# Two-block transformer, fp32, one core: passages between sublayers reordered, the mixer's last product held whole, gate units inside the attention

## The reference

```python
for l in range(DEPTH_2):
    x = x + 0.5 * rmsnorm_2(swiglu(rmsnorm_2(x, ffn1_pre_g[l]), w_ffn1_in[l], w_ffn1_out[l]), ffn1_post_g[l])
    h = rmsnorm_2(x, mix_pre_g[l])
    (z, xbc, dt_raw, rq, rk, rv, rg, aq, ak, av, gate) = jnp.split(h @ w_in[l], offsets, axis=-1)
    y_ssd = ssd_mixer(z, xbc, dt_raw, ...)
    y_ret = retention_mixer(rq, rk, rv, rg, ...)
    y_att = swa_sink_attention(aq, ak, av, ...)
    branch = jnp.einsum('blmc,mcd->blmd', ys, w_branch[l])
    gates = jax.nn.sigmoid((gate + b_gate[l]).reshape(bsz, L, N_BRANCH, D_MODEL))
    y = jnp.sum(gates * branch, axis=2) @ w_out[l]
    x = x + rmsnorm_2(y, mix_post_g[l])
    x = x + 0.5 * rmsnorm_2(swiglu(rmsnorm_2(x, ffn2_pre_g[l]), w_ffn2_in[l], w_ffn2_out[l]), ffn2_post_g[l])
```

## Time and profile before

| | |
|---|---|
| median of three executions | 2131.18 us |
| profiled execution | 2128.98 us, its span 2127.2 us |
| TensorE, matmuls | 1950.0 us busy, 92% |
| VectorE | 1150.1 us, 54% |
| ScalarE | 884.1 us, 42% |
| weights moved | 483 MB, 228 GB/s over the span |
| mean granted clock of TensorE | 0.946 |
| second block | from 621 us to the end |

### The profile page before, as it was taken

How to read it: one execution, slowest core, us unless ns; L and a number is a source line. 1 busy time by engine, 2 the same in 40 slices (tenths; PEclk the granted TensorE clock), 3 DMA queues, 4 the chain that set the end, 5 groups by cost and what they waited for, 6 DMA issues and landing times.

```text
span 2127.2 us, 29966 instructions
## 1 busy us (share of the span) xinstructions
PE 1950.0 (92%) x12346; PEld 1546.6 (73%) x12346; DVE 1150.1 (54%) x1583; ACT 884.1 (42%) x1288; POOL 47.5 (2%) x99
## 2 busy tenths in 40 slices
PE   7988766777779999999999999999999999999998
PEld 7873121121148887899899888898878999998887
DVE  5751100110137657477865676476674779656763
ACT  5521000000025444457744554354444577445552
POOL 0010000000000000000000100000000000001000
PEclk9988778777789999999999999999999999999999
DMA  7568999999995554543445455454545434355552
GB/s 280 194 262 327 421 421 421 421 421 421 421 368 176 213 186 171 184 158 120 149 159 180 180 193 185 177 178 182 195 178 186 170 120 149 140 181 188 188 191 87
DMA packets 66900, 486.05 MB, mean 228 GB/s; under 512 B 7424, under 2 KB 7424, under 8 KB 8544
## 3 DMA queue, kind: packets, MB, share of 16 engines
q1 hardware_dynamic: 65632, 476.25, 59.1%
q0 software_dynamic: 1152, 8.16, 1.0%
HBM read 483.33 MB, written 1.05 MB: 228 GB/s over the span
## 4 chain that ended last, share of the span: by engine, by line
PE 76%; DMA 10%; SPq 7%; DVE 3%; ACT 2%; issue 2%; POOL 1%; DVEq 0%; ACTq 0%; POOLq 0%
PE bank L1540 22%; PE bank L1555 12%; PE bank L1640 11%; DMA work<-in_w_experts 10%; PE bank L1873 8%; PE bank L1553 7%; SPq L1440 6%; PE bank L1569 3%; PE bank L1551 2%; PE bank L1368 2%; PE bank L1398 1%; PE bank L1421 1%; PE bank L1091 1%; ACT work L2319 1%; PE bank L2058 1%
## 5 line engine op out<-in xcount | busy, mean ns | idle before, releaser
L1518 DVE TENSOR_TENSOR ring_parts<-ring,work_parts 128x2048 fp32r<-128x2048 f32 x188 | 430.2, 2291 | 237.3 <-ACT work_parts L1511 223.1
L1511 ACT ACTIVATE work_parts<-ring 128x2048 fp32r<-128x2048 f32 x168 | 321.0, 1913 | 217.6 <-PE bank L1640 80.0
L1540 PE MATMUL bank<-work_parts 128*128 128x256 f32 x1376 | 317.6, 283 | 1.2 <-DVE ring_parts L1518 1.2
L1540 PE MATMUL bank<-rows_parts,work_parts 128*128 128x256 f32 x864 | 245.1, 284 | 0.0
L1540 PE MATMUL bank<-rows_parts,ring_parts 128*128 128x256 f32 x864 | 244.4, 283 | 0.0
L1540 PEld LDWEIGHTS bank<-work_parts 128*128 128x128 f32 x1376 | 238.9, 192 | 1.7 <-issue 1.5
L1555 PE MATMUL bank<-work_parts 128*128 128x512 f32 x840 | 213.2, 393 | 0.0
L1553 PEld LDWEIGHTS bank<-work_parts,ring_parts 128*128 128x128 f32 x1280 | 174.6, 190 | 12.3
L1398 PE MATMUL bank<-work 128*32 128x512 f32 x640 | 126.3, 886 | 59.2 <-DMA work<-in_w_experts 59.2
L1553 PE MATMUL bank<-work_parts,ring_parts 128*128 128x256 f32 x1280 | 178.5, 282 | 0.0
L1555 PEld LDWEIGHTS bank<-work_parts 128*128 128x128 f32 x840 | 150.1, 189 | 26.2
(11 more groups left out here) (387 smaller groups left out, 3150.7 us busy)
## 6 DMA issues: line engine op xcount, KB each, us to landing
ring<-in_w_layers SPq DMA_DIRECT2D x242, 1024.0 KB, 4.9
work<-in_w_experts SPq DMA_DIRECT2D x136, 1024.0 KB, 26.8
ring<-in_w_experts SPq DMA_DIRECT2D x48, 1024.0 KB, 26.7
ring<-in_w_first SPq DMA_DIRECT2D x16, 1024.0 KB, 5.5
columns<-in_w_experts SPq DMA_DIRECT2D x8, 1024.0 KB, 26.6
work<-in_post POOLq DMA_DIRECT2D x3, 1024.0 KB, 5.0
work<-in_second POOLq DMA_DIRECT2D x1, 2944.0 KB, 11.5
work<-in_first SPq DMA_DIRECT2D x1, 1805.5 KB, 11.3
```

Of the source, the lines that this page charges most:

```text
L1511: act.activation(his[j % len(his)], m.ring[U.slot(names[j])], ACT.Copy).then_inc(F["unit_hi"], 1)
L1518: dve.tensor_tensor(m.ring_r[slot], m.ring[slot], his[j % len(his)].bitcast(F32), ALU.subtract).then_inc(F["unit_lo"], 1)
L1540: mm = pe.matmul(out, w, x, start=k + n == 0, stop=k == KT - 1 and n == 2)
```

## The change

Six things are changed, in both layers of the second block:

- `bridge_vector`: rows of half 0 are scaled before bank (0,1) is read, and `next_columns(0)` comes before bank (1,1) is read; it came after x of half 1. One `OUT_ORDER` serves all three.
- `mx.out`: the mixer's last product holds all four units; half 0 is finished for both column halves, then half 1 (`out_rows`). Unit 0 of FFN 2 is taken apart after the passage and no longer before it.
- `mix_columns_vector`: the low part of a column is made straight from the bank by one fused instruction for each 128x128; the whole column is no longer stored, and the 16-row `dt` product, which read it, is split into three fp32r matmuls a step, with its weights taken apart too.
- The gate units `g.1.0` and `g.1.1` move into the two halves of the attention, and one unit more of the mixer's end is kept ahead (`END_AHEAD`), in four buffers instead of three.
- `turn_half(.., 1)`: the second half's transposes come later: in an FFN after 24 instead of 16 fp32 matmuls, in the mixer after 21 instead of 12 fp32r ones.
- `with_skips`: seven places of the job list stay empty in FFN 1, and the list's length is a multiple of eight.

```diff
+END_AHEAD = AHEAD_UNITS + 1
@@ place
+        if name is None:
+            continue
+SKIPPED = range(4, 18, 2)
+def with_skips(jobs):
+
+    return [n for job in jobs for n in ([None, job] if job in [f"f1.in.{i}.a" for i in SKIPPED] else [job])]
@@ LAYER_JOBS
-              + [f"ap.0.{kv}.{j}" for kv in range(2) for j in range(2)] + ["ao.0.0", "ao.0.1"]
-              + [f"ap.1.{kv}.{j}.{s}" for kv in range(2) for j in range(2) for s in range(2)] + ["ao.1.0", "ao.1.1"]
+              + [f"ap.0.{kv}.{j}" for kv in range(2) for j in range(2)] + ["g.1.0", "ao.0.0", "ao.0.1"]
+              + [f"ap.1.{kv}.{j}.{s}" for kv in range(2) for j in range(2) for s in range(2)] + ["g.1.1", "ao.1.0", "ao.1.1"]
+assert len(LAYER_JOBS) % BANKS == 0
+END_HOME = [(6, None, 4, 5)[j % 4] for j in range(14)] + [4, 3, 5, 6, None, 4]
@@ ffn_tensor
-    turn_half(pe, B, ps, m, F, f, 1)
     B.claim(pe, jobs[1])
-    whole_half(pe, B, U, ps, m, jobs[1], units[1], 0)
+    whole_half(pe, B, U, ps, m, jobs[1], units[1], 0, None, lambda: turn_half(pe, B, ps, m, F, f, 1))
@@ bridge_vector
-        if (n, t) == (1, 1):
+        if (n, t) == (0, 1):
             scaled(0)
+        elif (n, t) == (1, 1) and next_columns:
+            next_columns(0)
...
-    if next_columns:
-        next_columns(0)
     scaled(1)
@@ mix_tensor
+    def out_rows(held, ready):
+
+
+        for t in range(TT):
+            for n in range(2):
+                B.claim(pe, f"mx.out.{n}.{t}")
+        parts = {}
+        for u in range(2):
+            for n in range(2):
+                parts[n, u] = unit_parts(pe, m, U, F, "end", END_SPLIT, 16 + 2 * n + u, m.ehi_r, KT // 2)
+                part_rows(f"mx.out.{n}.0", parts[n, u], u, 0, held, ready if n == 0 else None)
+        for n in range(2):
+            part_rows(f"mx.out.{n}.1", parts[n, 0], 0, 1, held).then_inc(U.parts_sem, 1)
+            part_rows(f"mx.out.{n}.1", parts[n, 1], 1, 1, held)
...
-        mm = pe.matmul(ps[B.bank("dt")][0:16, 0:T], wdt[:, k, :], m.hT[:, k, :], start=k == 0, stop=k == KT - 1)
+        for n, (w, x) in enumerate(passes_of([w[:, k, :] for w in wdt], [x[:, k] for x in moving])):
+            mm = pe.matmul(split(ps[B.bank("dt")][0:16, 0:T], TT), w, x, start=k + n == 0, stop=k == KT - 1 and n == 2)
@@ attend
+        end_columns("g", 1, t, moving)
@@ mix_scalar
     for t in range(TT):
+        if t == 1:
+            gate(1, 0)
@@ mix_columns_vector
-        whole = dve.tensor_tensor(m.hT[:, c, tokens], half_of(ps, B, job, t), bc(m.lp["gmix"][:, c], [P, 2, P]), ALU.mult)
...
+        for k in range(2):
+            kk = 2 * i + k
+            ins = dve.scalar_tensor_tensor(out=m.mhlo_r[:, t, kk, :], in0=bank[:, k, :], scalar=m.lp["gmix"][:, kk:kk + 1],
+                                           in1=m.mh_r[:, t, kk, :].bitcast(F32), op0=ALU.mult, op1=ALU.subtract)
@@ mix_vector
+    bridge_vector(dve, m, ps, B, F, "mx", m.post[:, 0:D], 1.0, next_columns)
     for j in range(NEXT_UNITS["mx"]):
         next_unit(j)
-    bridge_vector(dve, m, ps, B, F, "mx", m.post[:, 0:D], 1.0, next_columns)
```

More of the change, by code:

```diff
@@ L1556, in wide_columns, with whole_half @@
         mm.then_inc(B.full(job), 1)
-def whole_half(pe, B, U, ps, m, job, unit, t, ready=None):
+def whole_half(pe, B, U, ps, m, job, unit, t, ready=None, between=None):
     pe.wait_ge(*U.landed(unit))
@@ L1564, in whole_half @@
     for c in range(2):
+        if between and c == 1:
+            between()
         out = ps[B.bank(job)][:, c * T + t * P:c * T + (t + 1) * P]
@@ L1721, in ffn_parts_scalar @@
         act.activation(m.both_r[:, :, tokens], m.hfull[:, :, tokens], ACT.Copy).then_inc(F["x_hi"], 1)
-OUT_ORDER = {"f1": ((0, 0), (1, 0), (0, 1), (1, 1)), "mx": ((0, 0), (0, 1), (1, 0), (1, 1)),
-             "f2": ((0, 0), (1, 0), (0, 1), (1, 1))}
+OUT_ORDER = ((0, 0), (1, 0), (0, 1), (1, 1))
 def squared(F, f, n, t):
-    return F.at(f"{f}.pss", OUT_ORDER[f].index((n, t)) + 1)
+    return F.at(f"{f}.pss", OUT_ORDER.index((n, t)) + 1)
 def bridge_scalar(act, m, ps, B, F, f, next_columns):
-    for n, t in OUT_ORDER[f]:
+    for n, t in OUT_ORDER:
         job = f"{f}.out.{n}.{t}"
@@ L1863, in mix_tensor, with part_rows @@
     moving = [x.rearrange("p t k n -> p k t n") for x in (m.mh_r, m.mhlo_r)]
-    def part_rows(job, parts, u, t, held, ready=None):
+    def part_rows(job, parts, u, t, held, ready=None, between=None):
         for k in range(KT // 2):
             kk = u * (KT // 2) + k
+            if between and k == KT // 2 - 1:
+                between()
             if ready and kk % 2 == 0:
@@ L1901, in split_rows_by_half @@
                     B.claim(pe, jobs[t])
-                mm = part_rows(jobs[t], parts[u], u, t, held, ready[t])
+                mm = part_rows(jobs[t], parts[u], u, t, held, ready[t], between if (t, u) == (0, 1) else None)
                 if (t, u) == (1, 0):
                     mm.then_inc(U.parts_sem, 1)
+    def out_rows(held, ready):
[10 more added lines that the diff above has]
+            part_rows(f"mx.out.{n}.1", parts[n, 1], 1, 1, held)
     turn_half(pe, B, ps, m, F, "mx", 0)
     split_rows_by_half(["rq.0", "rq.1"], "mx", MIX_SPLIT, 0, m.mhi_r, moving,
-                       [[F.at("mx.cols", 4 * t + i + 1) for i in range(4)] for t in range(TT)],
+                       [[F.at("mx.cols", i + 1) for i in range(4)], [B.drained(f"mx.n.{i}") for i in range(4)]],
                        lambda: turn_half(pe, B, ps, m, F, "mx", 1))
@@ L2081, in branch, with end_columns @@
             return
-        for n, (name, held) in enumerate((("g", moving), ("b", (m.yhi_r[b - 1], m.ylo_r[b - 1])))):
-            if n == 1:
-                pe.wait_ge(*F.at("end_lo", b))
-            for i in range(4):
-                job = f"{name}.{b}.{i}"
-                B.claim(pe, job)
-                parts = unit_parts(pe, m, U, F, "end", END_SPLIT, (b - 1) * 8 + n * 4 + i, m.ehi_r, KT)
-                split_columns(pe, B, ps, job, parts, held)
+        for i in range(2 if b == 1 else 0, 4):
+            end_columns("g", b, i, moving)
+        pe.wait_ge(*F.at("end_lo", b))
+        for i in range(4):
+            end_columns("b", b, i, (m.yhi_r[b - 1], m.ylo_r[b - 1]))
+    def end_columns(name, b, i, held):
+        job = f"{name}.{b}.{i}"
+        B.claim(pe, job)
+        parts = unit_parts(pe, m, U, F, "end", END_SPLIT, END_SPLIT.index(job), m.ehi_r, KT)
+        split_columns(pe, B, ps, job, parts, held)
     def attend(t):
@@ L2120, in mix_tensor @@
     branch(2)
-    summed = (m.yhi_r[0], m.sumlo_r)
-    split_rows(["mx.out.0.0", "mx.out.0.1"], "end", END_SPLIT, 16, m.ehi_r, summed,
-               [F.at("sum_lo", i + 1) for i in range(4)])
-    split_rows_by_half(["mx.out.1.0", "mx.out.1.1"], "end", END_SPLIT, 18, m.ehi_r, summed, (None, None), lambda: None)
+    out_rows((m.yhi_r[0], m.sumlo_r), [F.at("sum_lo", i + 1) for i in range(4)])
 def mix_unit_scalar(act, m, U, F, j):
@@ L2337, in end_unit @@
     def end_unit(j):
-        if j < len(END_SPLIT):
-            unit_hi(act, m, U, F, END_SPLIT, j, m.ehi_r)
-    act.wait_ge(*B.filled("b.0.1"))
+        if j >= len(END_SPLIT):
+            return
+        act.wait_ge(*B.filled(END_READ[j]))
+        act.wait_ge(*U.landed(END_SPLIT[j]))
+        act.activation(m.ehi_r[j], m.ring[U.slot(END_SPLIT[j])], ACT.Copy).then_inc(F["unit_hi"], 1)
     end_unit(0)
+    end_unit(1)
     for t in range(TT):
+        if t == 1:
+            gate(1, 0)
         for kv in range(2):
@@ L2349, in mix_scalar @@
                         turned_probs(act, m, ps, B, F, t, kv, j, s)
-    act.wait_ge(*B.filled("ap.1.1.1.1"))
-    end_unit(1)
+    end_unit(2)
     for b in (1, 2):
-        u = (b - 1) * 8 + AHEAD_UNITS
+        u = (b - 1) * 8 + END_AHEAD
         for i in range(4):
@@ L2361, in mix_scalar @@
                 act.activation(m.yhi_r[i], (m.yret, m.yatt)[i], ACT.Copy).then_inc(F["end_hi"], 1)
-            gate(b, i)
+            if (b, i) != (1, 0):
+                gate(b, i)
         for i in range(4, 8):
             end_unit(u + i)
-    for j in range(16 + AHEAD_UNITS, len(END_SPLIT)):
+    for j in range(16 + END_AHEAD, len(END_SPLIT)):
         end_unit(j)
+    bridge_scalar(act, m, ps, B, F, "mx", next_columns)
     for j in range(NEXT_UNITS["mx"]):
         next_unit(j)
-    bridge_scalar(act, m, ps, B, F, "mx", next_columns)
 def gates_of(m, i):
@@ L2849, in lay_out @@
     m.rv, m.aq, m.osqh = split(rv, TT), split(rv, KT), split(rv, 8)
+    m.wdt_r = [area_r[:, W.at + 1024 + i * P:W.at + 1024 + (i + 1) * P] for i in range(2)]
     rw = W.take(RET_H * 3 * P)
```

48 lines of the change are left out of this document (24 added, 24 removed).

## The result

| | before | after |
|---|---|---|
| median, six executions each | 2131.07 us (2127.7 to 2133.07) | 2111.71 us (2110.22 to 2115.69) |
| ratio | | 0.9913, 95% interval 0.990 to 0.9926 |
| profiled execution, its span | 2128.98, 2127.2 us | 2115.69, 2113.9 us |
| TensorE idle over 0.1 us at a time, behind the first transposes of the second block | 16.4 us | 7.2 us |
| low stretches (granted clock 0.50) between 650 us and the last product | 815.0 (6.8 us), 1183.7 (3.4), 1374.8 (3.4) | none |

A forecast was written before the change was run, and what follows sets the result against it. TensorE is busy 92%, so only idle gaps, low-clock stretches and matmul work could change the time. Terms summed to 9.0 us, 13.1 with the clock: 2131.18 to 2118; own range 2112 to 2122, 8 in 10 2111 to 2126.5.

The forecast's parts named there:

- into FFN 2, waits, two layers: Passage from mixer into FFN 2: idle falls from 2.51 to 0.55 us, 1.96 saved per layer, 3.9 in all.
- FFN 2 into FFN 1, waits: Layer 1's FFN 2 into layer 2's FFN 1: skipped places end the L1813 wait; idle 2.53 to 0.8, 1.7 us saved.
- mixer entry, waits, two layers: FFN 1 into the mixer: a new 1.8 us wait before the second transposes; 0.35 lost per layer, 0.7 in all.
- attention: Gate product between probability transposes and their product: 0.87 us gap goes, half 0's product shortens; 1.5 per layer, 2.9 saved.
- `dt` and what stands beside it: 16-row product: 24 fp32r matmuls replace eight fp32, 3.56 to between 2.7 and 3.0 us; 0.65 saved twice, 1.3.
- tail, behind the block: Very end: scaled rows stand ahead of two bank reads, x still waits for the root; 0.1 us lost.
- clock: Half-clock stretches after passages given back: 1.6 and 1.4 us, plus 1.1 of 2.5 at the mixer's entry; 4.1 together.
- The fit called "within 0.1": Mixer into FFN 2: half 1's scaled rows ready at T+6.4 us, its transposes asked for at T+6.5.
- the covered low part: Attention: VectorE's moved 2.29 us low part hides under the gate product; uncovered, its 2.29 would return in each layer.
- A: Rival, passages: idle goes but other passages, mostly the mixer's entry, take low-clock stretches; 9.0 saved, 2122 us; chance 0.21.
- B: Rival, five passages: half 1's x waits for columns, each losing another 1.5 us; 7.5 of 13.1 gone, 2125.5; chance 0.17.
- C: Rival, slower: low parts late at b.1.0 behind the attention, or held units late in the last product; 2136 and above; chance 0.04.

The follow-up runs named there:

- e3: Changed kernel with VectorE's old order in all five passages (half 0 scaled ahead of bank (1,1), next columns behind the update of x): 2128.12 us, ratio 0.9989.
- e2: Changed kernel with the mixer's last product in its old order (column half 0 for both token halves, then half 1), VectorE's order kept new: 2114.09 us, ratio 0.9929.
- e4: Changed kernel with the second half's transposes as early as before, ahead of the FFN's 17th product and the mixer's 13th: 2123.24 us, ratio 0.9968.
- e5: Kernel before the change plus only the empty places in FFN 1's job list: 2131.14 us, ratio 1.0004.
- e1: Changed kernel with gate products g.1.0 and g.1.1 back behind the attention, the earlier conversions kept: 2122.15 us, ratio 0.9967.
- e9: Kernel of e1 with VectorE's conversions of the second and third end unit moved behind the attention's copies: 2114.92 us, ratio 0.9931.
- e6: Kernel of e3 plus unread identity products on TensorE, meant to fill its waits before transposes and first products: 2122.75 us, ratio 0.9965.

## Why the prediction was right, and where its sizes were off

| term | forecast, us | measured, us |
|---|---|---|
| into FFN 2, waits, two layers | 3.9 | 5.4 |
| FFN 2 into FFN 1, waits | 1.7 | 1.9 |
| mixer entry, waits, two layers | -0.7 | -0.3 |
| attention | 2.9 | 2.9 |
| `dt` and what stands beside it | 1.3 | 2.4 |
| tail, behind the block | -0.1 | 0.0 (7.93 to 7.97) |
| clock | 4.1 | 5.4 |
| sum | 13.1 | 17.7 |

The first and third rows are twice what layer 2 shows by place, where the clock stayed up in both kernels. The clock's row is what layer 1 gained more than layer 2 in the same passage (2.29 + 0.14 at the mixer, 4.34 - 2.71 at FFN 2), and at FFN 1 the 3.23 by place less 1.87 of idle time.

The mechanism was right, and it is in part luck that the median fell into a stated range: the block saved a third more than the sum, nearly all sizes were off to the same side (into FFN 2 by 1.5, the clock by 1.3, `dt` and its neighbours by 1.1), and another 1.7 outside the block came on top.

**The bound.** That only gaps, clock and matmul work could move the time held. Of matmul work only `dt` and the first attention product (2.44 to 1.87, counted by the prediction) changed their length by more than 0.2 us.

**Into FFN 2.** The mechanism held, and e3 and e2 part it. The size was low by 0.75 per layer: of the 0.55 left idle, 0.15 behind the transposes and 0.35 for the columns of half 1 behind a conversion above all, nothing is there, and by place it gained 0.2 more than the idle time that went (2.71 beside 2.51). The fit called "within 0.1" was real: the rows of half 1 are ready at 1924.43, and the transposes are asked for 0.4 later (5.48 us behind the first product at 1919.34). e4 shows what that margin is worth.

**FFN 2 into FFN 1.** 0.66 of idle time stayed where 0.65 was forecast, and 0.15 more was counted that isn't there. But the prediction gave the skipped places the credit; e5 shows that alone they move the wait 0.7 us further on and save nothing.

**Mixer entry.** All four waits were named: 0.65, 0.7, 1.8 and 0.1 forecast, 0.6, 0.80, 1.29 and 0.17 measured. The 1.8 was too much by two things: the fused instruction takes 0.27 in a stream (2.16 for eight) and not 0.3, and TensorE asks 6.9 us behind T and not 6.6, since its first product started 0.1 later and 21 of them took 5.0. The place still lost 0.14 where the waits fell from 2.96 to 2.85; that 0.25 is no wait in the records.

**Attention.** 1.45 per layer for 1.5. The sentence on the covered low part ("its 2.29 would return in each layer") was right in direction and short: e1 gave 3.35 beside before, 2.2 of waiting and the rest the clock.

**The 16-row product.** 0.74 each (3.56 to 2.82, 0.117 a matmul), inside the bounds 2.7 to 3.0. The rest of that row was not forecast: 0.17 per layer at the transposes ahead of it, 0.1 per layer behind it, and a wait of 0.77 for a low part in layer 2 that became 0.40. By the Trainium skill (TensorE: Matmul & The Clock Gate, Back-to-back issue gap), whose figure for isolated matmuls of 256 columns is 262 cycles, 109 ns at 2.4 GHz, 24 would by estimate take 2.6. The trace's 2.82 stands between that and 24 at the 128-row spacing, 2.97.

**The clock** was 1.3 short, all at one place. I counted 1.1 of the 2.5 at the mixer entry, arguing by how much idle time is left. It came back whole (2.4). In the changed kernel that entry has 2.83 to 2.87 us of idle time in four pieces and never fell, in both layers of after, e1, e2 and e9; in e3 it has 2.85 and 2.86, as 0.89, 1.79 and 0.17, and fell in both. So the amount of idle time alone does not decide. That it matters how near the pieces lie together fits these ten, but it is not shown: the kernel before and e5 have 2.96 us in two pieces, nearer still, and fell in layer 1 and not in layer 2, and no run moved the pieces apart and left all else. That the idle time lets the clock fall is what e6 shows, in one profile. The Trainium skill (TensorE: Matmul & The Clock Gate, Why this matters for your kernels) warns only of longer gaps than these. The trace does not agree: e3 fell behind 0.89 and 1.79, and with these filled it did not.

**The rivals.** A did not happen (no low stretch). B did not: the only wait for half 1 is the one of 1.29 at the mixer entry, less than the forecast held already. C did not: no wait at b.1.0 or in the last product. The 4.4 us by which the start of the block moved between the two profiles is no part of any term, and 1.7 of the 19.4 lies outside the block or in the spread of the executions.

## What to carry to other kernels

Where an engine hands over between two stages, list its instructions in the order in which others wait for them, and put what the next stage's first matmul needs ahead of bookkeeping for the half that is needed later; without that order nearly the whole gain was gone here. What each part costs when it is taken away (e3 17.1, e4 10.9, e1 9.6, e2 1.6) adds up to 39 us, over twice the 17.7 that all of them gave: the parts lean on one another, and none of these numbers is what the part gives alone. An edit that moves work earlier on a helper engine needs its cover moved with it (the gates here). Short waits of TensorE can cost as much again in clock (2.72 of waiting cost 5.7 us in layer 1 of e3): remove them, or fill them with matmuls that fit, measured by their own duration.

## What the runs showed of the hardware that was not expected

- Equal idle time, different clock: 2.85 us in three pieces fell twice of two, 2.96 in two pieces twice of four (before, e5), 2.85 in four pieces never in eight passages. Waits behind which it fell each time: 3.08, 3.39, and 0.93 with 1.60 in either order; 0.88 or 1.35 alone never.
- A wait of 2.72 us let the clock fall in layer 1 of e3 and not in layer 2; before and e5 did the same with 0.61 and 1.90, and with 0.9 and 2.1 at the mixer entry. What differs between the layers stays open.
- Matmuls that nobody reads kept the clock at 1.00 behind waits where it fell without them (four passages of e3), also behind the one of 5.9 us at the start of the block, where it fell in every profile without enough of them.
- Such an fp32 product of 128x128 by 128 takes 0.228 us in a stream; a fused VectorE instruction of 128x128 out of PSUM 0.27.
